# First expert stage: expert weights loaded in rows of 16 KB a partition, tokens and hidden values taken in the same order

## The reference, cut to what matters

```python
def expert_block(args):
    idx, w, e = args
    xb = tok_pad[idx]
    hb = jax.nn.silu(xb @ ex_gate[e]) * (xb @ ex_up[e])
    return (hb @ ex_down[e]) * w[:, None]
```

## Time and profile before

| | us |
|---|---|
| median of 3 runs | 2442.31 |
| lowest, highest | 2436.27, 2442.68 |
| the profiled execution's own time | 2440.16 |
| its span, first to last instruction | 2438.4 |
| TensorE busy | 2179.7 (89% of the span) |
| VectorE busy, ScalarE busy | 707.8, 455.3 |
| moved by DMA | 511.99 MB, mean 210 GB/s |

### The profile page before, as it was taken

The page is one execution under the profiler, slowest core; times in us unless marked ns, Lnnn a source line. Parts: engine busy times, 40 slices in busy tenths (PEclk is TensorE's granted clock), DMA queues, the critical chain, the costliest instruction groups (busy, mean ns, idle before and its releaser), DMA issues.

```text
span 2438.4 us, 32561 instructions
## 1 busy us (share of the span) xinstructions
PE 2179.7 (89%) x14114; PEld 1494.9 (61%) x14114; DVE 707.8 (29%) x1511; ACT 455.3 (19%) x934; POOL 42.9 (2%) x32
## 2 busy tenths in 40 slices
PE   5899986489689999999989899999989989999998
PEld 3454663478555444444466588886767778847844
DVE  1285149745441111111043410002572230000001
ACT  3210125132031111111132510002222320000001
POOL 0000101100000000000000000000000000000000
PEclk9999966689889999999999999999988789999999
DMA  9352000000659999999872844326340138799796
GB/s 319 137 206 103 1 1 0 1 2 2 241 208 393 394 393 393 393 394 395 305 279 104 321 145 165 125 90 233 120 165 2 69 141 316 263 384 353 257 339 241
DMA packets 231400, 511.99 MB, mean 210 GB/s; under 512 B 8926, under 2 KB 32173, under 8 KB 230893
## 3 DMA queue, kind: packets, MB, share of 16 engines
q1 hardware_dynamic: 230512, 509.87, 56.9%
q10 hardware_dynamic: 765, 0.31, 0.0%
HBM read 509.11 MB, written 1.05 MB: 209 GB/s over the span
## 4 chain that ended last, share of the span: by engine, by line
PE 70%; DMA 14%; DVE 8%; SPq 3%; ACT 3%; issue 1%; POOL 0%; ACTq 0%; DVEq 0%; POOLq 0%
PE PS L377 33%; DMA work<-in_ex_up_dram 11%; PE PS L2100 6%; PE PS L2254 4%; PE PS L1957 3%; DMA work<-in_moe_w_gate_up_dram 3%; PE PS L2205 2%; SPq L1877 2%; PE PS L568 2%; PE PS L2021 1%; PE PS L2032 1%; PE PS L671 1%; PE PS L576 1%; PE PS L2121 1%; DMA work<-in_w_ada_dram 1%
## 5 line engine op out<-in xcount | busy, mean ns | idle before, releaser
L377 PE MATMUL PS<-hT,work 128*128 128x256 f32 x1456 | 326.9, 385 | 0.4 <-ACT hT L737 0.4
L377 PEld LDWEIGHTS PS<-hT,work 128*128 128x128 f32 x1456 | 278.7, 192 | 43.0 <-issue 2.8
L377 PE MATMUL PS<-work 128*128 128x256 f32 (+4 forms) x960 | 284.7, 457 | 9.9 <-DVE work L1706 5.7
L2100 PE MATMUL PS<-work,sq 128*64 128x512 f32 x1024 | 233.9, 611 | 25.5 <-DMA work<-in_ex_up_dram 24.2
L377 PEld LDWEIGHTS PS<-work 128*128 128x128 f32 (+2 forms) x960 | 177.8, 187 | 112.6 <-issue 76.9
L2100 PEld LDWEIGHTS PS<-work,sq 128*64 128x64 f32 x1024 | 82.8, 140 | 173.3 <-issue 173.3
L377 PE MATMUL PS<-sq,work 128*128 128x128 f32 x1408 | 163.3, 280 | 7.7 <-DMA work<-in_moe_w_gate_up_dram 7.7
L377 PEld LDWEIGHTS PS<-sq,work 128*128 128x128 f32 x1408 | 162.9, 197 | 9.6 <-issue 9.6
L2121 PE MATMUL PS<-work 128*64 128x512 f32 x512 | 113.4, 595 | 9.8 <-issue 9.8
L2254 PE MATMUL PS<-work 128*64 128x512 f32 (+1 forms) x352 | 114.4, 593 | 1.9 <-ACT work L2284 1.9
L2021 PEld LDWEIGHTS PS<-work,xc 128*128 128x128 f32 x768 | 87.9, 192 | 14.0 <-issue 13.9
(11 more groups left out here) (553 smaller groups left out, 2285.1 us busy)
## 6 DMA issues: line engine op xcount, KB each, us to landing
work<-in_ex_gate_dram SPq DMA_DIRECT2D x32, 2048.0 KB, 17.7
work<-in_ex_up_dram SPq DMA_DIRECT2D x32, 2048.0 KB, 19.3
work<-in_ex_down_dram SPq DMA_DIRECT2D x32, 2048.0 KB, 14.2
work<-in_moe_w_gate_up_dram SPq DMA_DIRECT2D x32, 2048.0 KB, 10.2
work<-in_ada_w_dram SPq DMA_DIRECT2D x24, 2048.0 KB, 8.5
work<-in_moe_w_down_dram SPq DMA_DIRECT2D x16, 2048.0 KB, 14.8
work<-in_w_ada_dram SPq DMA_DIRECT2D x12, 2048.0 KB, 9.0
work<-in_moe_w_gate_up_dram SPq DMA_DIRECT2D x16, 1536.0 KB, 13.3
```

The lines of the kernel that those rows point to most:

```text
L377: ins = pe.matmul(outp, lhs, rhs, start=n == 0, stop=n == len(pairs) - 1, **kw)
L2100: ins = pe.matmul(PS[pair[m], 6 + j, :], xs[:, k, pair[m]], unit(U[name] + 3 * m + j, KT, F)[:, k, :], start=k == 0, stop=k == KT - 1)
```

## The change

For moe1 alone, `ex_src` reads each matrix as `(p k) n -> p k n`: partition p gets the rows 8p to 8p+7 of gate and up (4p to 4p+3 of down), which lie one behind the other in HBM and make one run of 16 KB. So that the sums still pair the right features, the copy to `htok` reads every eighth column of the turned tokens: the 128 columns number k of `htok` now hold the features k, 8+k, 16+k, ... For the hidden features the same is done by the new helper `ptile`: where a tile of 128 hidden columns was a run, it is now every fourth column, as input of the four transposes in each round. The branch that isn't taken gets 16 transposes and two copies that put `hT` into the new order.

```diff
@@ -1848,9 +1848,15 @@
+        if name == "moe1":
+            return w.rearrange("(p k) n -> p k n", p=P)
         if what == "down":
             return w[t0 * P:(t0 + n) * P, :].rearrange("(k p) n -> p k n", p=P)
         return ktiles(w, c0 + t0 * P, n * P)
+
+    def ptile(name, t, n):
+
+        return slice(t, n * P, n) if name == "moe1" else slice(t * P, (t + 1) * P)
@@ -1931,7 +1937,7 @@
                                 ins = product(PS[:, 4 + (g - g0) % 4, j * N:(j + 1) * N],
-                                              [(w[:, k, t * P:(t + 1) * P], hT[:, k, :]) for k in range(KT)], paced=paced)
+                                              [(w[:, k, ptile(name, t, n)], hT[:, k, :]) for k in range(KT)], paced=paced)
@@ -2051,7 +2057,12 @@
     def as_they_lie_act(name):
         act.wait_ge(S["htok_turned"], tokens_turned[name])
-        act.activation(htok, PS[:, 0:4, :].rearrange("p (t b) n -> p t (b n)", t=2), ACT.Copy).then_inc(S["htok"], 1)
+        turned = PS[:, 0:4, :].rearrange("p (t b) n -> p t (b n)", t=2)
+        if name == "moe1":
+            act.activation(htok.rearrange("p t (k m) -> p t k m", m=P), turned.rearrange("p t (m k) -> p t k m", k=KT),
+                           ACT.Copy).then_inc(S["htok"], 1)
+        else:
+            act.activation(htok, turned, ACT.Copy).then_inc(S["htok"], 1)
@@ -2105,7 +2116,7 @@
             for f in range(FT):
-                ins = pe.transpose(PS[:, 6, f * P:(f + 1) * P], htk[:, f * P:(f + 1) * P], ident)
+                ins = pe.transpose(PS[:, 6, f * P:(f + 1) * P], htk[:, ptile(name, f, FT)], ident)
@@ -2353,7 +2364,14 @@
-        pe.wait_ge(S["rows_" + name], 2 * COUNT[name] // 4)
+        n_rows = 2 * COUNT[name] // 4
+        if name == "moe1":
+            for tt in range(2):
+                for k in range(KT):
+                    ins = pe.transpose(PS[:, 2 * tt + k // 4, (k % 4) * P:(k % 4 + 1) * P], htok[:, tt, k * P:(k + 1) * P], ident)
+            ins.then_inc(S["rowsum_" + name], 1)
+            n_rows += 1
+        pe.wait_ge(S["rows_" + name], n_rows)
@@ -2361,6 +2379,12 @@
+        if name == "moe1":
+            act.wait_ge(S["rowsum_" + name], 2 * COUNT[name] // 4 + 1)
+            for tt in range(2):
+                ins = act.activation(hT[:, :, tt * P:(tt + 1) * P],
+                                     PS[:, 2 * tt:2 * tt + 2, :].rearrange("p b (k n) -> p (b k) n", n=P), ACT.Copy)
+            ins.then_inc(S["rows_" + name], 1)
```

## The result

The changed kernel takes 2401.16 us (median of 4 runs, 2398.61 to 2403.30), the kernel before 2440.36 in the same comparison (4 runs, 2436.27 to 2442.68). The ratio is 0.9841 [0.9821, 0.9860], so the change gains 39.2 us where the prediction had 27.3; its 2413 is 12 us too high, and the lower end of its range, 2403, lies 1.8 us above the measured median.

A forecast was written before the change was run, and what follows sets the result against it. Full DMA engines were taken to bound the stage, with TensorE waiting for `ex_up`. -35.4 (waits, draining, lost clock) + 8.0 (strided transposes) + 0.1 (copy) = -27.3 us, from 2440.16 to 2412.9, left at 2413; range 2403 to 2428.

The forecast's parts named there:

- The bound and its size: Stage from slice 13 to 19: DMA engines full, TensorE waiting for `ex_up`; 35.4 us over TensorE's pace to win.
- The rate by run: Weight transfers: 387 GB/s at 2 KB, 410 at 4 KB; runs of 16 KB taken at 424, upper bound 430.
- Rivals 1 (long runs no faster than 410): Weight loads: 16 KB runs no faster than 4 KB ones, TensorE still waits a little; 2422 us, chance 0.12.
- 4 (collisions, 378): Weight loads: the 16 engines collide in HBM at power-of-two distances, 378 GB/s; 2460 us, slower, chance 0.06.
- 5 (cut into 2 KB): Weight loads: the queue cuts each run into 2 KB pieces again, downs fall to 387 GB/s; 2449 us, chance 0.03.
- The five clock falls: Five up products took 8.78 instead of 7.09 us, each directly after an `ex_up` wait of 2.4 us; 8.3 us.
- Rival 3: Stage's up products: the five clock falls are the chip's own rhythm and stay, 8.4 us; 2421 us, chance 0.12.
- SP's issues "growing as the backlog grows": Issuing a pair of gates takes 1.0 to 8.6 us, waiting for room behind earlier runs; would get no longer.
- So they come 7 us early: Last up loads arrive at 1163.9 us, TensorE wants them at 1170.9; no wait at the end down to 417 GB/s.
- The strided transposes: Four transposes a round (L2108) load weights at stride four: 0.50 us a round, 8.0 over the stage; bounds 0 and 0.66.
- rival 2: Transposes' weight loads: the stride is free, so only the 35.4 us count; 2405 us, chance 0.10.
- The copy to `htok`: ScalarE's copy reads every eighth number of PSUM: 0.1 us taken, far bound +1.9 us for twice the time.

## Why the prediction was right in kind and too small in size

**The bound and its size: right.** The DMA engines set the pace, the price was put at 35.4 us over TensorE's pace, and the stage lost 35.0. Runs of 4 and 8 KB and the kernel with fewer bytes come to the same from three sides. (The 35.0 has 0.5 us of stride in it.)

**The rate by run: right, and nearer the bound than the value taken.** I took 424 GB/s and kept 430 as an end; 428 came. Rivals 1 (long runs no faster than 410), 4 (collisions, 378) and 5 (cut into 2 KB) fall with it. The Trainium skill (DMA: Bandwidth & Descriptors, Why small descriptors are slow) has about 3 cycles fixed for a packet, from which 4% between 2 and 16 KB is an estimate. Measured are 387 and 428 GB/s, 10.6%; the measurement decides.

**The five clock falls: right.** They went with the waits, both here and in the kernel with fewer bytes; of the 11.2 us that the prediction gave to clock and draining together, 10.8 show in TensorE's busy time. Rival 3 falls. The prediction's words, each time directly after a wait of 2.4 us, are true of the falls and not of the waits: three of eight such waits had no fall behind them.

**SP's issues "growing as the backlog grows": only half.** They got no longer, as forecast. But with runs of 8 KB DMA bounds the stage's last rounds and a pair of gates is issued in 0.94 us still, and with fewer bytes in short runs the issue grows to 5.0 us without a wait. The number of runs has a part in it, and its length alone doesn't show whether a stage is bound by DMA.

**"So they come 7 us early": off.** It rested on rounds of 29.81 us. At 29.35 a round asks for 429 GB/s and gets 428, so there is next to no reserve, and at 422 GB/s waits are back (1.5 us with runs of 8 KB). No wait was left all the same.

**"The strided transposes" (0.50 us a round, 8.0 in all): this step failed.** On the path of the changed kernel, the chain of waits (start, us, what) shows:

```profile
972.79 0.47 PE PS L2119 x4
973.26 0.22 PE PS L2123 x2
```

In the earlier trace rows the four transposes take 0.44. The stride costs 0.03 us a round, 0.5 in the stage, not 8.0. The weight loads did get longer, though only to 202 ns where I expected 270:

```profile
L2119 PEld LDWEIGHTS PS<-consts,work x64: 195/202/212, 737.7 to 1178.3; 128*128 128x128 f32 x64
```

Two mistakes lie in the step. I priced the duration of a load that runs beside the matmul before it, when only the distance to the next instruction counts. And the pairs of the earlier trace rows that had a stride are plain matmuls, two records each, while the four instructions in question are transposes; the stride sweep shows that these two kinds answer differently (233 against 122 ns at stride 4). Nor did the lines of a pair compare like with like: L1457 works on four groups of rows by turns, L1479 on two, and their records follow one another after 28 and 29 ns, which the times in the earlier trace rows would have shown. The transposes' own far bound, 0, was in the text, and rival 2 is what happened. It was given 0.10.

The Trainium skill (Advanced Engine Details and Errata, Memory Cachelines) says that SBUF has lines of 16 bytes and that at least two hits on a line are needed for full speed. The plain matmuls agree (two float32 of a line are hit at stride 2: 118 ns; one at stride 4: 233), the transposes don't (122). The page gives no factor; with the doubling that the plain matmuls show, the forecast would have been about as wrong as with my step.

**The copy to `htok`: right.** It was given up to 0.1 us, and the far bound was 1.9:

```profile
L2062 ACT ACTIVATE xc<-PS x1: 1877/1877/1877, 696.2 to 696.2; 128x2048 f32<-128x2048 f32 x1
```

1877 ns, as in the earlier trace rows: reading every eighth number costs this copy nothing.

**The sum.** With the stride at 0.5 instead of 8.0 and the copy at 0 the prediction's own terms give -34.9, or 2405.3: the stage's -35.0, and the -35.1 over all runs. The first comparison shows 4.1 us more. Profiles of one and the same kernel differ by 8 us behind the stage, with TensorE's clock at half for more or less of it. In the profiled pair of the first comparison, 37.5 us apart, 35.0 lie in the stage, 2.9 behind it and -0.4 ahead of it. And the four runs of that comparison had a mean granted clock of 0.930 to 0.932, the twelve repeats 0.923 to 0.929. So I take the 4.1 for the clock outside the stage: luck of that comparison, without which the time would lie in the range, at its lower end. This is argued, not shown; no experiment held the rest of the kernel still.

## What to carry to other kernels

Where a stage is bound by weights from memory, load each tile in long runs (8 KB had most of the gain here), whatever order of rows this gives, and put the reordering where it is free: into a copy out of PSUM or into transposes, and not into the weight load of a plain matmul. Price an instruction by the distance to the next one in a row of the same kind, not by its duration. Once DMA and TensorE are both full, the next gain there needs fewer bytes and fewer products alike.

## What the hardware showed beyond that

- With a stride of 4 float32 numbers in its weight load a transpose is 12 ns slower than without (122 against 110), a plain matmul takes twice the time (233 against 112 for each record). A stride of 2 costs either 6 to 8 ns, and 8 is within 10 ns of 4.
- One core moves 428 GB/s over 300 us in runs of 16 KB. By the packets' times each run costs an engine about 10 ns beside its bytes.
- TensorE's granted clock fell from 2.4 to 1.2 GHz after five of the eight waits of 2.4 us in the kernel before, at a price of 1.7 us each. It didn't fall at the twelve waits of up to 1.2 us with runs of 4 KB. It fell once after a wait of 1.3 us, in the kernel with strided gathering matmuls, and not after the same wait in the changed kernel.
- SyncE's issue of a pair of gate loads took up to 8.9 us while the queue was backed up, and 0.9 us with the same bytes in an eighth of the runs.
